# Full-height attention products and a feed-forward split in three: a two-layer transformer kernel on one Trainium2 core

## The chip, the cores and the metric

The kernel runs on one core of one Trainium2 chip. The metric is device time in microseconds of one execution, the median of several runs. Lower is better. TensorE does the matmuls (PE in the profile, with its weight loads as PEld), VectorE (DVE), ScalarE (ACT) and GpSimd (POOL) do the elementwise work, SyncE (SP) issues most DMA transfers.

## The reference

Two transformer layers over 528 rows (16 meta rows and 512 sequence rows) of width 1024, all in f32. Layer 1 has two attention branches: a windowed one (8 heads of 64, 2 key heads) and a latent one in which a small "index" network scores all keys and the best 128 are kept. Layer 2 has a differential attention (4 heads, each the difference of two softmaxes over 64-wide keys, values 128 wide) and a windowed one (8 heads of 64, 2 key heads) in which every query also sees the meta keys. Each layer mixes its branches with gates, projects them, and ends in a SwiGLU feed-forward of width 2816. Cut to what matters:

```python
# layer 1, branch a: window of 128 keys, a sink logit per head, bias by distance
s = einsum('bnqhgd,bnkhd->bnhgqk', qb, kw) * 64 ** -0.5 + bias;  o = (softmax with sink) @ vw
# layer 1, branch b: index scores choose the keys of the latent attention
logits = einsum('bqhd,bsd->bqhs', qi, ik);  score = sum_h relu(logits) * iw;  sel = top_k(score)
s = einsum('bqhc,bqkc->bqhk', q_abs, c_sel) * 64 ** -0.5 + bias;  lat = softmax(s) @ c_sel;  o = lat @ w_uv
# layer 2, branch a: differential; branch b: window of 128 to both sides and the 16 meta keys
attn = softmax(q1 k1 + bias) - lam * softmax(q2 k2 + bias);  y = attn @ v
# end of each layer
h = h + mixed @ w_out
h = h + (silu(hn @ w_gate) * (hn @ w_up)) @ w_down        # width 2816 = 22 blocks of 128
```

## The kernel before

Activations lie transposed: 128 features by columns of rows. A weight product `product(name, i, b, x)` (from line 1509) makes 128 output features: for each of the 8 (or 11, 4, 2) blocks of the contraction it runs three fp32r passes of 512 columns, since both weights and activations are split in a high part and a residual (`wh`, `wl`; `hn[:, 0]`, `hn[:, 1]`). Each weight block passes a chain: SP loads it into `stage` (line 412, after `lo` says that the residual of the last one is done), ACT copies it to `wh` (line 605, `high`), DVE or POOL subtracts to get `wl` (lines 904, 516, `low`), PE multiplies, DVE takes the result out of PSUM and sets `ev`. There are two slots, b = 0 and 1, and the phases stand in order in `PHASES` (line 82). The tiles `stage`, `wh`, `wl`, `hid` are as wide as the longest contraction, `NFH` = 11 blocks.

The feed-forward of layer l runs in two parts, a and b, of 11 blocks of the 22 each: `gu{l}a` makes 11 blocks of the hidden `hid` (gate and up product of each), `dn{l}a` multiplies them with their part of the down weights and adds the 8 output chunks into `hT`; then the same for b. PE waits in the first product of a down phase for each `hid` block in turn (`made=(hid_lo, ...)`). In the last down phase, `dn1b`, every chunk is also turned into the next layer's input on ACT and DVE (line 1356, `end_chunk`: add, gain copy and two squares on ACT, residual, sum of squares), and only then DVE makes the residual of the next weights (`low_next`); `dn2b` does a shorter form of it (line 1489).

The attention stages run units, one per block of 128 queries and head (32 for both windows and the latent one, 16 for the differential). They are interleaved over units: in turn j PE makes the scores of unit j, transposes the softmax of unit j - 2, and multiplies the transposed softmax of unit j - 3 with the values; in the window stages, quarters of the gate products of the same layer (line 1652) go between.
Heads are 64 wide, so two heads share the 128 partitions of a tile. Scores of one head use 64 rows: `r = slice(...)` selects the lower or the upper half of both operands (lines 1700 to 1703 and 1876 to 1885; the index scores, lines 1627 to 1635; the differential scores, lines 1851 to 1856). The 16 meta keys are a chunk of their own with 16 rows in the value products (lines 1677, 1717, 1773, 1868, 1902), behind a 16-column transpose (line 1666). In window attention 2 a block that doesn't begin at the first key makes its scores in two products, 16 meta columns and the rest.

## Time and profile before

| | us |
|---|---|
| median of 3 runs | 1668.69 |
| lowest, highest run | 1652.63, 1673.7 |
| the profiled execution | 1652.3 |
| its span, first to last instruction | 1650.5 |
| PE busy in it | 1607.5 |
| DVE, ACT, POOL busy | 839.7, 535.2, 203.8 |

The time outside the span is 1.8 us. The mean granted clock of TensorE over the span is 0.993 of full speed. "Busy" for PE counts the modelled, overlapping durations of pipelined matmuls; the distance between two starts is a better measure of what one takes. Idle "issue" is time in which an engine waited for nothing that the profile shows.

### The profile page before, as it was taken

The page shows a single profiled execution, that of the slowest core. Times are in us where ns is not written, and L with a number is a line of the kernel's source. Part 1 is how long each engine was busy: PE and PEld are TensorE (multiplying, and loading weights), DVE is VectorE, ACT ScalarE, POOL GpSimd, SP SyncE. Part 2 cuts the span into 40 slices and gives each one's busy share as a digit, 9 for nine tenths or more (in the row PEclk, how much of TensorE's full clock was granted, in tenths as well). Part 3 has the DMA queues.
Part 4 walks back from the last instruction along what each step waited for, and adds up shares of the span by engine and source line. Part 5 has one row for each costly group of instructions (what it writes and reads, how often), then busy time and mean ns, then how long its engine had stood idle before and what let it go on. Part 6 is the DMA issues. An engine that isn't in the chain of part 4 may idle for free.

```text
span 1650.5 us, 21586 instructions
## 1 busy us (share of the span) xinstructions
PE 1607.5 (97%) x7698; PEld 1273.5 (77%) x7698; DVE 839.7 (51%) x1579; ACT 535.2 (32%) x978; POOL 203.8 (12%) x140
## 2 busy tenths in 40 slices
PE   7899999999999999999999999999999999999997
PEld 6766776777878888888899777677777888888886
DVE  5277796436555533555554382332465554245543
ACT  4123443433322322223321363443333322122232
POOL 2222221003000000000002372221220000000000
PEclk9999999999999999999999999999999999999999
DMA  5832220003333332333232201111133333323331
GB/s 142 204 106 60 57 65 20 1 14 107 90 90 102 99 105 77 89 98 104 81 87 78 62 14 52 52 42 36 51 102 98 94 89 109 94 77 99 95 105 69
DMA packets 250508, 132.62 MB, mean 80 GB/s; under 512 B 20938, under 2 KB 247366, under 8 KB 250447
## 3 DMA queue, kind: packets, MB, share of 16 engines
q1 hardware_dynamic: 248318, 123.92, 26.5%
q0 software_dynamic: 2048, 7.77, 1.8%
q8 instruction: 37, 0.61, 0.2%
q14 instruction: 25, 0.20, 0.0%
q10 hardware_dynamic: 80, 0.14, 0.0%
HBM read 129.67 MB, written 6.38 MB: 82 GB/s over the span
## 4 chain that ended last, share of the span: by engine, by line
PE 91%; DVE 5%; DMA 2%; issue 1%; ACT 1%; POOL 0%; SPq 0%; DVEq 0%; ACTq 0%
PE psL L1529 59%; PE psL L1652 12%; PE psS L1529 4%; PE psL L1773 2%; PE psS L1902 2%; PE psT L1663 2%; PE psS L1703 1%; PE psS L1751 1%; DMA stage<-in_w_in 1%; PE psS L1717 1%; PE psL L1868 1%; PE psS L1885 1%; DMA xin<-in_x 1%; DVE W L1158 1%; PE psT L1666 1%
## 5 line engine op out<-in xcount | busy, mean ns | idle before, releaser
L1529 PE MATMUL psL<-hn,wh 128*128 128x512 f32 x1664 | 525.4, 397 | 5.2 <-POOL wl L516 5.0
L1529 PEld LDWEIGHTS psL<-hn,wh 128*128 128x128 f32 x1664 | 313.1, 189 | 82.6 <-POOL wl L516 5.2
L605 ACT ACTIVATE wh<-stage 128x1024 fp32r<-128x1024 f32 (+3 forms) x234 | 239.8, 1025 | 308.8 <-PE psL L1529 199.4
L1529 PE MATMUL psL<-hn,wl 128*128 128x512 f32 x832 | 329.8, 396 | 0.0
L904 DVE TENSOR_TENSOR wl<-stage,wh 128x1024 fp32r<-128x1024 f32 (+1 forms) x152 | 198.8, 1308 | 95.2 <-ACT wh L605 90.3
L1529 PE MATMUL psL<-hid,wh 128*128 128x512 f32 x704 | 221.3, 395 | 0.0
L516 POOL TENSOR_TENSOR wl<-stage,wh 128x1024 fp32r<-128x1024 f32 (+2 forms) x82 | 156.1, 1904 | 522.6 <-ACT wh L605 522.6
L1529 PEld LDWEIGHTS psL<-hn,wl 128*128 128x128 f32 x832 | 156.8, 188 | 36.5
L1652 PE MATMUL psL<-hn,wh 128*128 128x512 f32 x512 | 173.0, 419 | 0.0
L1529 PEld LDWEIGHTS psL<-hid,wh 128*128 128x128 f32 x704 | 132.3, 188 | 32.0
L1529 PE MATMUL psL<-hid,wl 128*128 128x512 f32 x352 | 139.2, 396 | 0.0
L1652 PEld LDWEIGHTS psL<-hn,wh 128*128 128x128 f32 x512 | 87.4, 189 | 35.7 <-issue 22.1
L1652 PE MATMUL psL<-hn,wl 128*128 128x512 f32 x256 | 101.1, 395 | 0.0
L794 ACT ACTIVATE hid<-ft 128x512 f32 (+1 forms) x44 | 27.8, 632 | 208.6 <-DVE ft L1321 208.6
L1529 PE MATMUL psS<-hn,wh 128*128 128x264 f32 x448 | 86.3, 294 | 0.7 <-DVE hn L949 0.7
L1529 PE MATMUL psL<-mix,wh 128*128 128x512 f32 x256 | 80.7, 396 | 0.9 <-DVE wl L904 0.9
L1338 DVE TENSOR_TENSOR hT<-hT,psL 128x512 f32 (+1 forms) x32 | 22.0, 688 | 112.5 <-PE psL L1529 112.5
L1529 PEld LDWEIGHTS psL<-hid,wl 128*128 128x128 f32 x352 | 66.1, 188 | 16.0
L1158 DVE CUSTOM_DVE_ANT_0 W3b<-psS,biasW,sinkb 128x272 f32<-128x272 f32 (+1 forms) x32 | 18.1, 567 | 112.1 <-PE psS L1885 82.6
L790 ACT ACTIVATE ft<-ft 128x512 f32<-128x512 f32 x44 | 27.8, 632 | 146.0 <-DVE ft L1313 146.0
L1529 PEld LDWEIGHTS psS<-hn,wh 128*128 128x128 f32 x448 | 71.8, 194 | 2.5 <-issue 1.2
L1529 PE MATMUL psS<-hn,wl 128*128 128x264 f32 x224 | 64.8, 289 | 0.0
(356 smaller groups left out, 2038.0 us busy)
## 6 DMA issues: line engine op xcount, KB each, us to landing
stage<-in_w_in SPq DMA_DIRECT2D x54, 512.0 KB, 3.8
stage<-in_w_ffn_gate SPq DMA_DIRECT2D x22, 512.0 KB, 3.8
stage<-in_w_ffn_up SPq DMA_DIRECT2D x22, 512.0 KB, 3.8
stage<-in_w_ffn_down SPq DMA_DIRECT2D x16, 704.0 KB, 4.5
stage<-in_w_ff_gate SPq DMA_DIRECT2D x22, 512.0 KB, 3.8
stage<-in_w_ff_up SPq DMA_DIRECT2D x22, 512.0 KB, 3.8
stage<-in_w_ff_down SPq DMA_DIRECT2D x16, 704.0 KB, 4.6
stage<-in_w_out SPq DMA_DIRECT2D x16, 512.0 KB, 3.8
```

The lines of the kernel that those rows point to most:

```text
L516: pool.tensor_tensor(wl[:, b, 0:n], stage[:, b, 0:n], wh[:, b, 0:n].bitcast(F32), ALU.subtract).then_inc(lo[b], 1)
L605: act.activation(wh[:, b, 0:n], stage[:, b, 0:n], ACT.Copy).then_inc(hi[b], 1)
L790: act.activation(ft[:, 1, :], ft[:, 0, :], ACT.Tanh, scale=0.5).then_inc(t_ok, 1)
L794: act.activation(hid[:, 0, bass.ds(i, 1), :], ft[:, 4, :], ACT.Copy).then_inc(hid_hi, 1)
L904: v.tensor_tensor(wl[:, b, 0:n], stage[:, b, 0:n], wh[:, b, 0:n].bitcast(F32), ALU.subtract).then_inc(lo[b], 1)
L1158: dv.link(v.tensor_tensor_reduce(out=tile, in0=scores, in1=bias, scale=1.0, scalar=least, op0=ALU.add, op1=ALU.max, accum_out=mx[:, col:co ...
L1338: v.tensor_tensor(hT[:, n, :], hT[:, n, :], psL[:, b, :], ALU.add).then_inc(ev[b], 1)
L1529: ins = pe.matmul(dst, w[:, b, k * P:(k + 1) * P], x[:, part, k, c0:c1], start=k + n == 0, stop=k == kc - 1 and n == 2)
L1652: ins = pe.matmul(psL[:, b, :], w[:, b, k * P:(k + 1) * P], hn[:, part_, k, META:], start=k + n == 0, stop=k == KD - 1 and n == 2)
L1663: ins = pe.transpose(psT[:, 0, n * P:(n + 1) * P], tile[:, col:col + P], ident[:])
L1773: ins = pe.matmul(psL[:, 0, 0:P], cn[0:w, c, :], pt, start=n == 0, stop=n == len(parts) - 1)
L1902: ins = pe.matmul(psS[:, 2 * (i % 2) + 1, h * HD:(h + 1) * HD], pt, vbn[0:w, c, h // 4 * HD:h // 4 * HD + HD], start=n == 0, stop=n == len ...
```

## The change

Scores use 128 rows. Where two key heads shared a tile (`akT`, `kbT`, and `ikT` with the same index key in both halves), the keys are now stored twice: `akz[:, g]` holds key head g in its own half of the partitions and zeros in the other half, so that the product over all 128 partitions of the query tile, which holds two heads, gives the score of one head. DVE makes these tiles, per g with a zero fill of one half and a product or copy of the other. The differential scores stay as they are.

The meta chunk of the value products uses 128 rows: the value tiles' row block of the meta keys is zero beyond row 16 (for layer 2 POOL fills it, for layer 1 that stood already), the transposed softmax too (four fills on DVE, before each stage), and the transpose takes 128 columns. In window attention 2 the meta keys also stand behind the last key, so that block 2 gets its scores in one product.

The feed-forward has three parts a, b, c of 8, 8 and 6 blocks, `NFH` is 8, and the last down phase is `dn{l}c`.

The core of the diff:

```diff
-NFH = FF // P // 2
+FPARTS = (8, 8, 6)
+NFH = max(FPARTS)
...
+def feed_forward(l):
+    return [f for ab, n in zip("abc", FPARTS) for f in ((f"gu{l}{ab}", 2 * n, KD, 1), (f"dn{l}{ab}", KD, n, 1))]
+
+def before_part(l, part):
+    return (l - 1) * sum(FPARTS) + sum(FPARTS[:part])
...
-        w, m, bias = (0, n * P, META + P) if i == 0 else (META, 0, 0)
+        w, m, bias = (0, n * P, META + P) if i == 0 else (0, n * P, META) if i == 2 else (META, 0, 0)
...
-        akT, o = at("akT", [P, NKEY], o)
+        akz, o = at("akz", [P, 2, NKEY], o)
-        ikT, o3 = at("ikT", [P, NKEY], o3)
+        ikz, o3 = at("ikz", [P, 2, NKEY], o3)
-        kbT, o = at("kbT", [P, NKEY], o)
+        kbz, o = at("kbz", [P, 2, NKEY + META], o)
...
             pool.wait_ge(ev[1], PAIR0["kv2"] + 1)
+            pool.memset(van[:, MC, :], 0.0)
+            pool.memset(vbn[:, MC, :], 0.0).then_inc(zeros, 1)
...
+            def split_keys(name, i, b, dst, again=0):
+                done(name, i, b)
+                for g in range(2):
+                    mine, other = slice(g * HD, (g + 1) * HD), slice((1 - g) * HD, (2 - g) * HD)
+                    v.memset(dst[other, g, :], 0.0)
+                    if again:
+                        v.tensor_copy(dst[mine, g, NKEY:NKEY + again], psS[mine, 2 * b, 0:again])
+                    ins = v.tensor_tensor(as_halves(dst[mine, g, 0:NKEY], NKEY), psS[mine, 2 * b:2 * b + 2, 0:NKEY // 2],
+                                          as_halves(Rk[mine, :], NKEY), ALU.mult)
+                ins.then_inc(ev[b], 1)
...
-                take_keys("kv1", i, 0, keys[2 * i])
                 if i:
+                    split_keys("kv1", i, 0, akz)
                     low_next("kv1", i, True)
+                else:
+                    take_keys("kv1", i, 0, keys[2 * i])
...
-            for n, dst in enumerate((cT, ikT)):
-                v.tensor_copy(dst[:, META:NKEY], psS[:, n, :])
-                v.tensor_copy(dst[:, 0:META], psT[:, 0, n * META:(n + 1) * META])
+            v.tensor_copy(cT[:, META:NKEY], psS[:, 0, :])
+            v.tensor_copy(cT[:, 0:META], psT[:, 0, 0:META])
+            for g in range(2):
+                mine, other = slice(g * HD, (g + 1) * HD), slice((1 - g) * HD, (2 - g) * HD)
+                v.memset(ikz[other, g, :], 0.0)
+                v.tensor_copy(ikz[mine, g, META:NKEY], psS[mine, 1, :])
+                v.tensor_copy(ikz[mine, g, 0:META], psT[mine, 0, META:2 * META])
...
+            v.memset(PTa[:, :, NEAR:], 0.0)
...
+            v.memset(PT[:, :, NB * P:], 0.0)
...
+            v.memset(PT2[:, :, NB * P:], 0.0)
...
+            v.memset(PTb[:, :, WIN2:], 0.0)
...
-                    pe.matmul(psS[:, 2 * (j % 2), 0:W], aqT[r, h % 4, i * P:(i + 1) * P], akT[r, k0:k0 + W], start=True, stop=True).then_inc(p["s"], 1)
+                    pe.matmul(psS[:, 2 * (j % 2), 0:W], aqT[:, h % 4, i * P:(i + 1) * P], akz[:, h // 4, k0:k0 + W], start=True, stop=True).then_inc(p["s"], 1)
...
-                        pe.transpose(psT[0:META, 1, 0:P], tile[:, col:col + META], ident[:])
+                        pe.transpose(psT[:, 1, 0:P], tile[:, col:col + P], ident[:])
...
-                        found.append((pt[0:META, pt.shape[-1] - P:], c, META))
+                        found.append((pt[:, pt.shape[-1] - P:], c, P))
...
-                products(f"dn{l}a", hid, made=(hid_lo, NFH * (2 * l - 2)))
-                products(f"gu{l}b", hn)
-                products(f"dn{l}b", hid, made=(hid_lo, NFH * (2 * l - 1)))
+                products(f"dn{l}a", hid, made=(hid_lo, before_part(l, 0)))
+                for part, ab in enumerate("bc", 1):
+                    products(f"gu{l}{ab}", hn)
+                    products(f"dn{l}{ab}", hid, made=(hid_lo, before_part(l, part)))
...
+                    elif k0 + W == NKEY and mcol == W:
+                        ins = pe.matmul(psS[:, 2 * (j % 2), 0:W + META], q, k[:, k0:NKEY + META], start=True, stop=True)
```

The index scores and the scores of window attention 2 change in the same way as the line of `akz`; the loops of SP, ACT and DVE over the parts follow `FPARTS`.

## Rows read from the trace of the kernel before

**Rows 1.** The page: busy time of the engines, and the chain by engine

```profile
PE 1607.5 (97%) x7698; PEld 1273.5 (77%) x7698; DVE 839.7 (51%) x1579; ACT 535.2 (32%) x978; POOL 203.8 (12%) x140
...
PE 91%; DVE 5%; DMA 2%; issue 1%; ACT 1%; POOL 0%; SPq 0%; DVEq 0%; ACTq 0%
```

**Rows 2.** Busy by stretch: length; PE, PEld, DVE, ACT, POOL; granted clock, DMA share, GB/s

```profile
0.00:129.40 129.40, 107.74 (x546) 86.21 (x546) 69.71 (x152) 38.96 (x65) 32.17 (x41) 0.95 0.58 148
129.40:223.30 93.90, 93.90 (x428) 69.73 (x428) 70.66 (x235) 38.53 (x100) 26.39 (x11) 0.98 0.22 57
223.30:257.00 33.70, 33.70 (x163) 25.95 (x161) 32.25 (x80) 13.31 (x33) 9.61 (x4) 1.00 0.21 55
277.50:357.00 79.50, 76.55 (x497) 60.50 (x496) 33.07 (x133) 36.04 (x127) 0.00 (x0) 1.00 0.00 1
937.40:998.40 61.00, 55.93 (x371) 42.05 (x371) 48.93 (x152) 37.82 (x97) 31.97 (x24) 1.00 0.03 10
998.40:1158.00 159.60, 159.60 (x775) 114.78 (x775) 44.29 (x138) 62.51 (x159) 34.60 (x15) 1.00 0.16 47
466.00:764.00 298.00, 297.89 (x1279) 239.91 (x1278) 143.16 (x166) 78.44 (x93) 0.00 (x0) 1.00 0.33 95
```

**Rows 3.** Timeline, a unit of window attention 1: start, length, engine, line, idle before

```profile
180.71 0.55 PE L1717 MATMUL psS<-avn,PTa 128*128 128x64 f32 x4
...
181.19 0.70 PE L1703 MATMUL psS<-akT,aqT 64*128 64x256 f32 x2
181.81 0.30 PEld L1652 LDWEIGHTS psL<-hn,wh 128*128 128x128 f32 x2 [0.33 <-issue]
...
182.38 0.39 PE L1652 MATMUL psL<-hn,wl 128*128 128x512 f32 x1
```

**Rows 4.** Timeline of PE, a unit of latent attention (x10 is 2 of 16 rows, 8 of 128)

```profile
336.75 0.33 PE L1763 MATMUL psL<-wuv,lat 128*128 128x64 f32 x2
337.01 1.57 PE L1773 MATMUL psL<-PT,cn 16*128 16x128 f32 x10
338.42 0.61 PE L1751 MATMUL psS<-cT,qabs 128*128 128x264 f32 x2
338.87 0.28 PE L1752 MATMUL psS<-selm,identb 128*128 128x264 bf16 x1
```

**Rows 5.** Timeline of PE, the eight 128-row value passes of the same unit alone

```profile
337.43 1.16 PE L1773 MATMUL psL<-PT,cn 128*128 128x128 f32 x8
```

**Rows 6.** Timeline of PE, a unit of window attention 2 (x6 is 2 of 16 rows, 4 of 128)

```profile
1032.07 0.39 PE L1652 MATMUL psL<-hn,wl 128*128 128x512 f32 x1
1032.39 1.02 PE L1902 MATMUL psS<-vbn,PTb 16*128 16x64 f32 x6
...
1034.75 0.40 PE L1652 MATMUL psL<-hn,wl 128*128 128x512 f32 x1
```

**Rows 7.** Timeline of PE, first two index scores, and differential scores on both halves

```profile
111.63 0.52 PE L1635 MATMUL psS<-ikT,iqT 64*128 64x144 f32 x4 [0.90 <-DVE wukT L1114]
...
969.83 0.72 PE L1855 MATMUL psS<-kaT,qaT 64*128 64x264 f32 x4
```

**Rows 8.** Timeline of DVE, end of gu1b and first chunk of dn1b

```profile
764.42 0.69 DVE L1319 TENSOR_TENSOR ft<-psL,Rk 128x512 f32<-128x512 f32 x1 [0.79 <-PE psL L1529]
...
767.39 0.91 DVE L1261 MEMSET sqacc<- 128x1024 f32 x1 [0.16 <-issue]
...
772.18 0.69 DVE L1338 TENSOR_TENSOR hT<-hT,psL 128x512 f32 x1 [2.20 <-PE psL L1529]
...
775.18 1.23 DVE L1267 TENSOR_TENSOR sqacc<-sqacc,tmp 128x1024 f32<-128x1024 f32 x1 [0.21 <-ACT tmp L816]
776.37 1.62 DVE L904 TENSOR_TENSOR wl<-stage,wh 128x1408 fp32r<-128x1408 f32 x1
```

**Rows 9.** Timeline of DVE, first chunk of dn2b

```profile
1583.17 0.69 DVE L1338 TENSOR_TENSOR hT<-hT,psL 128x512 f32 x1 [2.39 <-PE psL L1529]
...
1586.61 1.62 DVE L904 TENSOR_TENSOR wl<-stage,wh 128x1408 fp32r<-128x1408 f32 x1 [1.10 <-ACT wh L605]
```

More of the change, by code:

```diff
@@ L38 @@
 FF = 2816
-NFH = FF // P // 2
+FPARTS = (8, 8, 6)
+assert sum(FPARTS) * P == FF
+NFH = max(FPARTS)
 HD = 64
@@ L453, in layer_rest @@
                         load(f"out{l}", i, b, by_rows(wo), i * (2 * P) + b * P)
-                for half, ab in enumerate("ab"):
+                for part, ab in enumerate("abc"):
+                    f0 = sum(FPARTS[:part])
                     with sp.Fori(0, PAIRS[f"gu{l}{ab}"]) as i:
-                        load(f"gu{l}{ab}", i, 0, by_rows(wg), i * P + half * NFH * P)
-                        load(f"gu{l}{ab}", i, 1, by_rows(wu), i * P + half * NFH * P)
+                        load(f"gu{l}{ab}", i, 0, by_rows(wg), i * P + f0 * P)
+                        load(f"gu{l}{ab}", i, 1, by_rows(wu), i * P + f0 * P)
                     with sp.Fori(0, PAIRS[f"dn{l}{ab}"]) as i:
                         for b in range(2):
-                            load(f"dn{l}{ab}", i, b, by_rows(wd, half * NFH, NFH), i * (2 * P) + b * P)
+                            load(f"dn{l}{ab}", i, b, by_rows(wd, f0, FPARTS[part]), i * (2 * P) + b * P)
             layer_rest(1, win1, 1476, t["w_branch_a"][0], t["w_branch_b"][0], t["w_out"][0],
@@ L803, in _ @@
             squares_and_gain("out1", 0, ROW["ffn_norm_g"])
-            swiglu("gu1a", 0, 1)
+            swiglu("gu1a", before_part(1, 0), 1)
             only_high("dn1a")
-            swiglu("gu1b", NFH)
-            name = "dn1b"
+            swiglu("gu1b", before_part(1, 1))
+            only_high("dn1b")
+            swiglu("gu1c", before_part(1, 2))
+            name = "dn1c"
             def chunk1(i, b):
@@ L861, in _ @@
             squares_and_gain("out2", 2, ROW["norm_ffn_2"])
-            swiglu("gu2a", 2 * NFH, 1)
+            swiglu("gu2a", before_part(2, 0), 1)
             only_high("dn2a")
-            swiglu("gu2b", 3 * NFH)
-            name = "dn2b"
+            swiglu("gu2b", before_part(2, 1))
+            only_high("dn2b")
+            swiglu("gu2c", before_part(2, 2))
+            name = "dn2c"
             def chunk2(i, b):
@@ L1030, in take_scaled @@
                 v.scalar_tensor_tensor(out=dst, in0=psL[:, b, :], scalar=scale, in1=by, op0=ALU.mult, op1=ALU.mult).then_inc(ev[b], 1)
-            keys = [bkvT[:], ikwT[:], akT[:], avT[:]]
+            def split_keys(name, i, b, dst, again=0):
[8 more added lines that the diff above has]
+                ins.then_inc(ev[b], 1)
+            keys = [bkvT[:], ikwT[:], None, avT[:]]
             for i in range(2):
@@ L1350, in _ @@
             out_project(1, 0, 0, ROW["ffn_norm_g"])
-            swiglu("gu1a", 0, (2, 3))
+            swiglu("gu1a", before_part(1, 0), (2, 3))
             down("dn1a")
-            swiglu("gu1b", NFH)
+            swiglu("gu1b", before_part(1, 1))
+            down("dn1b")
+            swiglu("gu1c", before_part(1, 2))
             def end_chunk(i, b):
                 n = 2 * i + b
-                add_down("dn1b", i, b)
+                add_down("dn1c", i, b)
                 gain_low(n, 2 * i + (KD + b), g12, 0)
@@ L1362, in end_pair @@
             def end_pair(i, last):
-                low("dn1b", i, 1)
+                low("dn1c", i, 1)
                 end_chunk(i, 0)
-                low_next("dn1b", i, last)
+                low_next("dn1c", i, last)
                 end_chunk(i, 1)
@@ L1369, in _ @@
             meta_low(2)
-            pairs("dn1b", end_pair)
+            pairs("dn1c", end_pair)
             low("kv2", 0, 1)
@@ L1386, in _ @@
             v.wait_ge(R_ok, 4)
-            keys = [kaT[:, c, :] for c in range(4)] + [vaT[:, c, :] for c in range(4)] + [kbT[:], vbT[:]]
+            keys = [kaT[:, c, :] for c in range(4)] + [vaT[:, c, :] for c in range(4)] + [None, vbT[:]]
             for i in range(PAIRS["kv2"]):
@@ L1390, in _ @@
                     low("kv2", i, 1)
-                take_keys("kv2", i, 0, keys[2 * i])
+                if i == PAIRS["kv2"] - 1:
+                    split_keys("kv2", i, 0, kbz, META)
+                else:
+                    take_keys("kv2", i, 0, keys[2 * i])
                 if i:
@@ L1409, in _ @@
             v.wait_ge(nat_t, 2)
+            v.wait_ge(zeros, 2)
             for h in range(4):
@@ L1484, in _ @@
             out_project(2, 2, 2 * KD, ROW["norm_ffn_2"])
-            swiglu("gu2a", 2 * NFH, (4, 5))
+            swiglu("gu2a", before_part(2, 0), (4, 5))
             down("dn2a")
-            swiglu("gu2b", 3 * NFH)
+            swiglu("gu2b", before_part(2, 1))
+            down("dn2b")
+            swiglu("gu2c", before_part(2, 2))
             def last_pair(i, last):
-                low("dn2b", i, 1)
-                add_down("dn2b", i, 0)
+                low("dn2c", i, 1)
+                add_down("dn2c", i, 0)
                 add_squares(3, 2 * i, sqacc[:, 0, :], sq[:])
-                low_next("dn2b", i, last)
-                add_down("dn2b", i, 1)
+                low_next("dn2c", i, last)
+                add_down("dn2c", i, 1)
                 add_squares(3, 2 * i + 1, sqacc[:, 0, :], sq[:])
             clear_squares()
-            pairs("dn2b", last_pair)
+            pairs("dn2c", last_pair)
             new_rms(5)
```

25 lines of the change are left out of this document (11 added, 14 removed).

## Prediction

> **What bounds the kernel now.** I read the page's busy shares and its chain first [rows 1]: the reader is to see that the chain that ended last is TensorE (PE) for 91%, so the time is mostly the sum of what PE streams plus its switching. Then the busy table by stage [rows 2]. In the sliding-window attention of layer 1 (129 to 257 us) and of layer 2 (998 to 1158 us) PE is busy for the whole stretch, in the latent attention (277 to 357) for 76.55 of 79.50 us, in the feed-forward for all of it. The differential attention (937 to 998) is mixed: PE 55.93, DVE 48.93 of 61.00 us. In the last quarter of window attention 1 DVE is busy for 32.25 of 33.70 us, a second bound close behind PE. "Busy" hides stalls, since matmul ends are modelled, so the third view is the timeline of single units [rows 3 to 6], where the distance between starts is what counts.
>
 So the other seven take 0.78, 0.11 us each. Two 264-column score passes of 128 rows take 0.45 (338.42 to 338.87), 0.22 each. A 512-column pass is 298 us / 1279 = 0.23, in the stretch from 466 us [rows 2]. These are the unstalled prices.
>
> Now a unit of window attention 1 [rows 3]: four value passes, two 64-row score passes, two gate passes take 180.71 to 182.38 = 1.67 us. Unstalled they are 0.39 + 0.44 + 0.46 = 1.29 (the first 64-column value pass takes 0.06, the other three 0.11: the weight load sets it). The rest, 0.38 us, is two switches of height: the weight load of the other height comes late, and its row puts the idle 0.33 down to "issue", not to a semaphore. A 16-row meta chunk in the latent stage [rows 4]: two output passes, two meta passes, eight value passes take 336.75 to 338.42 = 1.67; unstalled 12 x 0.11 less 0.05 = 1.27; the switches cost 0.40. Window attention 2 has both [rows 6]: from the last gate pass at 1032.07 to the third one after it at 1034.75 is 2.68; unstalled 0.23 (gate) + 0.06 + 7 x 0.11 (second meta pass, values, 16-column scores) + 2 x 0.22 + 2 x 0.23 = 1.96. Saved per unit: 0.72.
>
> **Gains, stage by stage.** Columns and passes stay, only the height changes, and score passes of 64 and of 128 rows stream alike.
> - Window attention 1: 24 units x 0.38 = 9.1, and 0.34 (0.72 less 0.38) for the meta chunk of the first 8 = 2.7. In the last 8 units DVE leaves at most 33.70 - 32.25 = 1.4 of their 3.0; I take 1.0. Sum 12.8.
> - Latent: 32 x 0.40 = 12.8; its early units already wait on others in part (PE 76.55 of 79.50), so I take 11.
> - Window attention 2: 32 x 0.72 = 23.0, with DVE at 44.29 of 159.60 and ACT at 62.51. Block 2's meta columns join its main score product: two 16-column passes x 0.11 x 8 units = 1.8. Sum 24.8.
> - Differential: its scores keep half height; only the meta chunk changes, 16 x 0.40 = 6.4, between 0 (DVE sets the pace, at 80% and in bursts) and 6.4: I take 3.
>
> Gains: 51.6 us.
>
> **Costs.**
> (a) The index scores lose an overlap. Four 64-row passes of 144 columns on opposite halves take 0.52 us busy [rows 7]. At full height they go end to end: later by 0.2 in the small block, by 0.9 (four passes of 0.22) in the large. ReLU on ACT takes the units one by one anyway, so between 0 and 4 x 0.6 = 2.4; I take 0.5, as the switches around the three q products go too.
> (b) The padded index keys are made on DVE between the key transposes and the first index score, where PE waits (idle 0.90, released by DVE) [rows 7]: two zero fills of 528 columns and one more copy of 512. A fill of 1024 columns takes 0.91 [rows 8], so 0.47 each; the copy, like the 512-column add at 772.18, 0.69: 1.6 us, all on the path.
> (c) The window keys of layer 1 get the same and push one weight residual 1.5 us later, so also the reload of its buffer; PE still has a product to run then: between 0 and 1.5, I take 0.5. Layer 2's are behind a product of PE: 0; without that cover, 1.6.
> (d) Four zero fills of 256 strided columns, 0.25 each on DVE at the head of a stage: 0.8 together. The two on POOL run after its long wait, ahead of work that needs ACT first: 0, without that cover about 1.
> (e) FFN. Weights, passes and bytes are the same in all; per layer there are 8 more accumulations into hT (0.69 each [rows 8]; DVE is busy 143 of 298 us), 8 more loads on SP and conversions on ACT, all of narrower blocks, and one more wait of PE for a last hid chunk. That chunk is ready some 3.0 us after the last up product (764.42 to the fill at 767.39) [rows 8], and PE needs it 3 x 0.23 x (n - 1) after it: 4.8 us for n = 8, 3.45 for n = 6: no stall. What does not shrink is the end of the layer. In the last down part of layer 1 DVE does per chunk [rows 8]: add (772.18), wait for ACT's copy and two squares (till 775.18), add squares, residual of the next weights (from 776.37, 1.62 us for 1408 columns). At 768 columns the residual lies between a 512-column pass (0.69) and a 1024-column one (1.23): 0.96. The cycle is then 776.37 - 772.18 + 0.96 = 5.15 us, while PE needs 18 x 0.23 = 4.14 (it was 5.8 against 7.6). DVE becomes the bound: 1.0 us x 6 chunks, 1.0 for the second chunk (its residual stands behind the 0.91 fill), 0.6 at the end: 8 us; late next is the head of the keys of layer 2. In layer 2 only one square is taken [rows 9]: 1586.61 - 1583.17 = 3.44, less 0.5 for ACT's narrower conversion, plus 0.96 = 3.9, below 4.14; the way back to PE adds some 0.14 a chunk, and the fill 0.9: 2 us. Together 10, between 4 and 16.
>
> Costs: 0.5 + 1.6 + 0.5 + 0.8 + 10 = 13.4 us.
>
> **Sum.** 51.6 - 13.4 = 38 us. The profiled execution took 1652.3, so 1614 on its own terms. It stands at the low end of the three runs, whose median, 1668.7, is 1.0% above it; from there the sum is 1631. Two of the three runs lie high, so I take **1626 us**. The gain at best: 51.6 + 3.4 + 1.8 less costs of 7.4 = 49; at worst 38 - 3 - 6 - 2 = 27. The case's own range is 1604 to 1645.
>
> **A rule that speaks against it.** Half-height passes on opposite halves overlap: four of 264 columns in the differential stage take 0.72 busy, where two of full height take 0.61 [rows 4, 7]. The Trainium skill, "TensorE: Matmul & The Clock Gate", Part 3 (Packing small matmuls), says that matmuls in distinct row groups run concurrently, and advises to place small contractions so; the trace agrees where such products are neighbours. By that rule the index scores would lose their whole overlap: an estimate of 2 us more than I count, a gain of 36. In the window stages no two score products are neighbours [rows 3, 6], and nothing is lost.
>
> **Rivals.**
> 1. *Other engines take the gain.* DVE or ACT sets the pace in more units (window 1 from its third block, all of differential, early latent: 3 + 3 + 5 us), and the short down part loses 1.7 instead of 1.0 a chunk (6 us): 38 - 17 = 21, 1631 to 1648. For it: 32.25 of 33.70. Against: PE busy throughout elsewhere. Chance 0.16.
> 2. *The change doesn't do what it says:* the gaps around short products are semaphore waits, so full height leaves them and only the costs remain, 1666 to 1682. Against: inside one accumulation, with no wait between its chunks, the 16-row passes take 0.21 instead of 0.11 [rows 4, 5]. Chance 0.05. The skill's same page, Part 2 (LDWEIGHTS), lets a load run ahead into the background weights, by which there would be nothing to gain; the rows show this only between equal heights.
> 3. *Slower, by the clock.* PE would idle more in the latent and differential stages. If the granted clock fell there from 2.4 to 1.2 GHz, as parts of the first 129 us must have (mean 0.95) [rows 2], their PE time (66 + 53 us after the change) would double: +119 - 38, over 1725; from some 70 us at half clock on it is slower by 2%. Against: both stages stand at 1.00 now with 3 and 5 us idle. Chance 0.03.
> 4. *More is gained:* differential gives 6, the FFN ends cost 3: 48 us, 1604 to 1621. Chance 0.08.
>
> **How the numbers follow.** A difference of 2% (33 us) is about what a measurement of this kernel can tell from none. My case has 0.68; of its span 27 to 49 about a sixth lies under 33, so 0.57 faster, 0.11 the same. With rival 4, 0.65 faster; with rivals 1 and 2, 0.32 the same; 0.03 slower. The range 1602 to 1650 takes in my case at either level of the runs, rivals 4 and 1, and leaves out rivals 2 and 3 and some ends.
>
> **What would show it.** Right: window 2 units 0.7 us shorter with no "issue" idle ahead of the first gate weight load; meta passes 0.11 apart; DVE without gaps in the last eight units of window 1; PE idle about 1 us per chunk in dn1c, waiting for wl, little in dn2c; the first index score 1.6 us later after the transposes. Wrong: 0.2 us gaps that stay at full height, a lower clock in the latent stage, or PE waiting in the 8-wide parts.

## The result, and the profile after

The changed kernel takes 1617.74 us (median of 4 runs, 1616.44 to 1618.78); the kernel before took 1669.21 us beside it (4 runs, 1652.63 to 1673.7). The ratio is 0.9709, 95% interval 0.9642 to 0.9776: faster by more than 2%, as forecast, and inside the range of 1602 to 1650, 8 us below the 1626 that I named. The profiled execution of the changed kernel took 1618.78 us, its span is 1617.0. Against the profiled execution of before the gain is 33.5 us, where I had summed 38; between the medians it is 51.5 us. The two differ for a reason that I had not foreseen (experiments 1, 4 to 7 and 9 to 12).

The page of the changed kernel: busy time by engine, and the chain that ended last [rows 1].

```profile
PE 1563.0 (97%) x7682; PEld 1271.6 (79%) x7682; DVE 861.4 (53%) x1627; ACT 537.4 (33%) x994; POOL 204.1 (13%) x142
...
PE 84%; DVE 9%; issue 2%; DMA 2%; ACT 2%; POOL 0%; SPq 0%; DVEq 0%; ACTq 0%
```

PE still sets the end, with 16 instructions fewer and 44.5 us less "busy"; DVE's share of the chain went from 5% to 9%. Where, the table by stage tells (columns as in [rows 2]); the last two lines are the feed-forward of layer 1, ahead of its last down part and in it.

```profile
131.80:214.50 82.70, 82.70 (x432) 69.37 (x433) 71.83 (x237) 37.60 (x100) 26.38 (x11) 1.00 0.25 65
214.50:252.00 37.50, 34.86 (x178) 28.68 (x177) 35.66 (x87) 14.15 (x35) 9.56 (x4) 1.00 0.20 56
269.80:340.00 70.20, 65.38 (x478) 54.28 (x478) 32.88 (x133) 35.12 (x124) 0.00 (x0) 1.00 0.00 1
928.20:986.00 57.80, 51.22 (x370) 41.89 (x370) 49.49 (x152) 37.78 (x97) 30.51 (x24) 1.00 0.04 10
986.00:1124.00 138.00, 137.80 (x760) 114.94 (x758) 45.79 (x139) 61.38 (x157) 35.93 (x15) 1.00 0.19 54
530.50:776.90 246.40, 246.40 (x1057) 198.74 (x1056) 111.85 (x130) 61.04 (x72) 0.00 (x0) 1.00 0.32 93
776.90:817.10 40.20, 35.69 (x146) 26.38 (x144) 28.48 (x35) 19.94 (x31) 0.00 (x0) 1.00 0.27 79
```

In the last units of window 1 DVE is busy for 35.66 of 37.50 us and PE no longer for the whole stretch; the latent stage leaves PE 4.8 us idle (it was 2.95); the last down part leaves it 4.5. Window 2 is as full of PE as before, and 21 us shorter.

Between the first score of window 1 and the first latent one each of the two profiled executions has a stretch at half clock, at different places, and in the table below they nearly cancel. In the kernel before it is at the head of window 1:

```profile
130.50:133.90 3.40, 3.40 (x9) 2.10 (x8) 2.45 (x13) 0.69 (x3) 2.22 (x1) 0.50 0.01 2
```

In the changed kernel it is as long and begins at 252.6 us, at the tail of window 1.

The same comparison from one stage's first product to the next one's, read from the two timelines. The third column is what my sum gives, each cost in its place:

| stretch | before us | after us | difference | my sum |
|---|---|---|---|---|
| start to first score of window 1 | 129.38 | 131.76 | +2.4 | +2.1 |
| to first latent score | 148.19 | 138.03 | -10.2 | -12.1 |
| to last latent score | 73.25 | 66.59 | -6.7 | -10.8 |
| branch, FFN 1, to first differential score | 586.60 | 591.84 | +5.2 | +8 |
| to first score of window 2 | 60.98 | 57.83 | -3.2 | -2.8 |
| to its last score | 156.88 | 135.81 | -21.1 | -24.6 |
| FFN 2, to the end | 495.20 | 495.12 | -0.1 | +2 |
| sum | 1650.5 | 1617.0 | -33.5 | -38 |

Timeline of PE in the changed kernel: a unit of window 1 [rows 3], of the latent stage [rows 4] and of window 2 [rows 6].

```profile
170.45 0.55 PE L1763 MATMUL psS<-avn,PTa 128*128 128x64 f32 x4
170.84 0.65 PE L1749 MATMUL psS<-akz,aqT 128*128 128x256 f32 x2
171.14 0.81 PE L1699 MATMUL psL<-hn,wh 128*128 128x512 f32 x2
171.78 0.40 PE L1699 MATMUL psL<-hn,wl 128*128 128x512 f32 x1
...
331.26 0.33 PE L1809 MATMUL psL<-wuv,lat 128*128 128x64 f32 x2
331.43 1.33 PE L1819 MATMUL psL<-PT,cn 128*128 128x128 f32 x10
332.60 0.39 PE L1797 MATMUL psS<-cT,qabs 128*128 128x264 f32 x1
...
1007.83 0.40 PE L1699 MATMUL psL<-hn,wl 128*128 128x512 f32 x1
1008.07 0.78 PE L1950 MATMUL psS<-vbn,PTb 128*128 128x64 f32 x6
1008.68 0.35 PE L1932 MATMUL psS<-kbz,qbT 128*128 128x16 f32 x2
1008.87 0.68 PE L1933 MATMUL psS<-kbz,qbT 128*128 128x256 f32 x2
1009.20 0.81 PE L1699 MATMUL psL<-hn,wh 128*128 128x512 f32 x2
1009.85 0.40 PE L1699 MATMUL psL<-hn,wl 128*128 128x512 f32 x1
```

The window 1 stretch, four value passes to the third gate pass, is 170.45 to 171.78 = 1.33 us (1.67 before); the latent one 331.26 to 332.60 = 1.34 (1.67); the window 2 one 1007.83 to 1009.85 = 2.02 (2.68), for the two excursions in it. Each excursion to another height and back had cost 0.33 us, in all three stages. I had 0.38, 0.40 and 0.36. The weight load of the first gate pass, which had 0.33 us of "issue" idle ahead of it [rows 3], has none:

```profile
170.78 0.30 PEld L1749 LDWEIGHTS psS<-akz,aqT 128*128 128x128 f32 x2
171.11 0.41 PEld L1699 LDWEIGHTS psL<-hn,wh 128*128 128x128 f32 x2
```

What PE and its weight loads waited for in the changed kernel: in start-up, at the end of window 1, in the latent stage (two lines) and in the last down part of layer 1 (us in total, times, longest).

```profile
PE psS L1682 <- DVE wukT L1150: 3.1, 1, 3.1
...
PE psL L1699 <- DVE tmp L1177: 1.9, 1, 1.9
...
PE psT L1713 <- ACT PT L732: 1.9, 5, 0.8
...
PEld psT L1713 <- ACT W L716: 5.6, 10, 1.0
...
PE psL L1577 <- DVE wl L922: 4.1, 7, 0.9
```

The first was 0.90 before [rows 7]: the padded index keys' fills and copy, 2.2 us. The second is new: DVE at the tail of window 1. The third and fourth are the latent stage's waits for ACT: PE for its copies of the transposed weights (0.9 us in one wait before), the weight loads of the transposes for its exponentials (1.7 us in three before). The fifth is the short down part. Timeline of DVE there, one chunk [rows 8]:

```profile
795.00 1.23 DVE L1305 TENSOR_TENSOR sqacc<-sqacc,tmp 128x1024 f32<-128x1024 f32 x1 [0.23 <-ACT tmp L832]
796.14 0.95 DVE L922 TENSOR_TENSOR wl<-stage,wh 128x768 fp32r<-128x768 f32 x1
797.01 0.68 DVE L1376 TENSOR_TENSOR hT<-hT,psL 128x512 f32 x1
799.03 0.75 DVE L1310 SCALAR_TENSOR_TENSOR hn<-hT,g,hn  x1 [1.33 <-ACT hn L830]
800.01 1.23 DVE L1305 TENSOR_TENSOR sqacc<-sqacc,tmp 128x1024 f32<-128x1024 f32 x1 [0.23 <-ACT tmp L832]
```

From one chunk to the next it takes 800.01 - 795.00 = 5.0 us (I had 5.15), where PE needs 4.14. The residual of 768 columns takes 0.95 (I had 0.96).

### The profile page after: what moved, and what is told of

It is laid out like the page before. It is cut to its first block, busy times and chain, and to the rows that moved or that the text cites. A ratio compares the mean times of both kernels' runs of the same rounds, so it can differ in the third digit from the quotient of the medians.

```text
span 1617.0 us, 21794 instructions
## 1 busy us (share of the span) xinstructions
PE 1563.0 (97%) x7682; PEld 1271.6 (79%) x7682; DVE 861.4 (53%) x1627; ACT 537.4 (33%) x994; POOL 204.1 (13%) x142
## 4 chain that ended last, share of the span: by engine, by line
PE 84%; DVE 9%; issue 2%; DMA 2%; ACT 2%; POOL 0%; SPq 0%; DVEq 0%; ACTq 0%
PE psL L1577 57%; PE psL L1699 10%; PE psS L1577 5%; PE psT L1710 1%; PE psL L1819 1%; PE psS L1950 1%; DVE W L1194 1%; PE psS L1797 1%; DMA stage<-in_w_in 1%; DMA xin<-in_x 1%; DVE acc L1188 1%; PE psT L1713 1%; DVE st L1187 1%; PE psS L1749 1%; DVE wl L922 1%
## 5 line engine op out<-in xcount | busy, mean ns | idle before, releaser
L1577 PEld LDWEIGHTS psL<-hn,wh 128*128 128x128 f32 x1664 | 313.3, 189 | 82.3 <-POOL wl L528 5.3
L619 ACT ACTIVATE wh<-stage 128x1024 fp32r<-128x1024 f32 (+3 forms) x250 | 243.2, 973 | 341.9 <-PE psL L1577 238.4
L1699 PEld LDWEIGHTS psL<-hn,wh 128*128 128x128 f32 x512 | 92.2, 190 | 21.2 <-issue 2.0
L808 ACT ACTIVATE hid<-ft 128x512 f32 (+1 forms) x44 | 27.8, 632 | 210.2 <-DVE ft L1359 210.2
L1376 DVE TENSOR_TENSOR hT<-hT,psL 128x512 f32 (+1 forms) x48 | 32.9, 686 | 104.3 <-PE psL L1577 104.3
L804 ACT ACTIVATE ft<-ft 128x512 f32<-128x512 f32 x44 | 27.8, 632 | 150.0 <-DVE ft L1351 150.0
```

The source lines that it names most:

```text
L619: act.activation(wh[:, b, 0:n], stage[:, b, 0:n], ACT.Copy).then_inc(hi[b], 1)
L804: act.activation(ft[:, 1, :], ft[:, 0, :], ACT.Tanh, scale=0.5).then_inc(t_ok, 1)
L808: act.activation(hid[:, 0, bass.ds(i, 1), :], ft[:, 4, :], ACT.Copy).then_inc(hid_hi, 1)
L1376: v.tensor_tensor(hT[:, n, :], hT[:, n, :], psL[:, b, :], ALU.add).then_inc(ev[b], 1)
L1577: ins = pe.matmul(dst, w[:, b, k * P:(k + 1) * P], x[:, part, k, c0:c1], start=k + n == 0, stop=k == kc - 1 and n == 2)
L1699: ins = pe.matmul(psL[:, b, :], w[:, b, k * P:(k + 1) * P], hn[:, part_, k, META:], start=k + n == 0, stop=k == KD - 1 and n == 2)
```

## The experiments

Twelve kernels. The executions of some of them fall into two groups, one with a mean granted clock of about 0.99 and one of about 0.98, 18 us apart in the kernel before. Of 52 executions of the kernel before beside these runs, 36 stand at 0.98 (median 1671) and 16 at 0.99 (median 1653). The profiled execution of before belongs to the second group, the median of its runs to the first.

### 1. The kernel before, once more

The file is unchanged.

> The kernel before, unchanged, as a yardstick of what two runs of one program differ by. Its four runs so far span 1652.6 to 1673.7 us, those of the changed kernel 1616.4 to 1618.8. Theory: the profiled execution (1652.3) is a lucky one and the others lose about 16 us in some stage; then a trace of a 1669 us execution shows that stage, most likely as a stretch with the granted clock at half or as a stall ahead of the first scores. Rival: the spread is spread over all stages, nothing to be seen. Ratio 1.00 in both.

Measured: 1671.65 us, ratio 1.0033 (0.9975 to 1.0091); 8 of 10 executions at the lower clock, and the profiled one is among them. Busy by stretch (columns as in [rows 2]): the first 5.9 us of the latent stage and the 37.5 us after them, first in this execution,

```profile
278.40:284.30 5.90, 4.69 (x31) 3.33 (x30) 3.14 (x17) 2.92 (x14) 0.00 (x0) 1.00 0.00 0
284.30:321.80 37.50, 37.50 (x135) 29.62 (x135) 10.23 (x46) 10.52 (x47) 0.00 (x0) 0.50 0.00 1
```

then in the execution of before that stands ahead of the prediction,

```profile
277.50:283.40 5.90, 4.69 (x31) 3.33 (x30) 3.14 (x17) 2.92 (x14) 0.00 (x0) 1.00 0.00 0
283.40:320.90 37.50, 37.50 (x235) 28.88 (x236) 17.39 (x73) 18.27 (x72) 0.00 (x0) 1.00 0.00 1
```

and in the changed kernel.

```profile
275.70:313.20 37.50, 36.13 (x259) 28.95 (x258) 18.99 (x80) 19.27 (x74) 0.00 (x0) 1.00 0.01 1
```

The same program did the same 31 matmuls in the same 5.90 us; then in one execution the granted clock was 0.50 (1.2 GHz) for 37.5 us and 135 matmuls got done, in the other it stayed at 1.00 (2.4 GHz) and 235 did. First to last latent score takes 89.90 us in the one and 73.25 in the other: 16.65 us, most of the 18 between the groups. The changed kernel's four executions stand at 0.991 to 0.995. So the 51.5 us between the medians are 35 at an equal clock (1653 to 1617.7) and 16 from the clock, if the executions without a profile lost their time in the same place, as their clock and time suggest. The next question was which part of the change holds the clock.

### 2. The feed-forward parts alone

The kernel before with the three parts and their loops; scores over 64 rows and meta chunks of 16 as they were.

```diff
-NFH = FF // P // 2
+FPARTS = (8, 8, 6)
+NFH = max(FPARTS)
```

> The kernel before with the feed-forward in parts of 8, 8 and 6 alone; keys, meta chunk and transposes as before. Theory (the short last part makes DVE the bound in dn1c): slower than before by 6.5 us in layer 1 and 1.4 in layer 2 as the changed kernel's trace has it (40.1 and 35.0 us for 144 passes that stream in 33.6), sum 8 us, ratio 1.005. Rival (the split costs nothing, and the gain in attention is smaller than I think): 0 to 2 us, ratio 1.000.

Measured: 1669.47 us, ratio 1.003 (0.9972 to 1.0088). The share of low executions was smaller (5 of 10, against 15 of 25 of the kernel before beside it, a difference that chance can make), which hides the cost; at equal clock it is 1659 against 1653 and 1678 against 1671: 6 to 7 us. By stage: from last latent to first differential score 593.0 (586.6 before), window 2's last score to the end 496.4 (495.2). I had 8 + 2.

### 3. The narrow part first

```diff
-FPARTS = (8, 8, 6)
+FPARTS = (6, 8, 8)
```

> The changed kernel with the parts in the order 6, 8, 8, so that the last down part is 8 wide. Theory: DVE's cycle per chunk is 5.15 + 0.27 = 5.4 us, PE needs 24 x 0.23 = 5.5, so PE no longer waits: 6 to 8 us less than the changed kernel, 1610 us. The 6-wide part at the front has no extra work on DVE and loses nothing. Rival (each change from one part to the next costs, not the width of the last): as the changed kernel, 1617.

Measured: 1612.87 us, ratio 0.9662 (0.9591 to 0.9733), 4.9 us below the changed kernel (the spans of the two profiles: 1612.3 and 1617.0). Layer 1's stretch is 587.9 us instead of 591.8, layer 2's 493.6 instead of 495.1 (586.6 and 495.2 in the kernel before, the same sum within 0.3). The page's group for the hid products shows the wait gone; in this run, and then in the changed kernel:

```profile
L1577 PE MATMUL psL<-hid,wh 128*128 128x512 f32 x704 | 221.7, 396 | 0.2
```

```profile
L1577 PE MATMUL psL<-hid,wh 128*128 128x512 f32 x704 | 222.5, 397 | 4.7 <-DVE wl L922 4.7
```

The feed-forward's cost is the order of its parts, not their number: a last part of 6 blocks gives PE too little work for DVE's cycle of 5.0 us, one of 8 (24 x 0.23 = 5.5 us of PE a chunk) gives enough, though its residual of 1024 columns takes DVE 1.22 us instead of 0.95. There DVE waits for PE, in run 3:

```profile
788.44 1.22 DVE L922 TENSOR_TENSOR wl<-stage,wh 128x1024 fp32r<-128x1024 f32 x1
789.90 0.69 DVE L1376 TENSOR_TENSOR hT<-hT,psL 128x512 f32 x1 [0.24 <-PE psL L1577]
```

### 4. Meta chunks back at 16 rows in all four stages

The four zero fills of the transposed weights go too.

```diff
-pe.transpose(psT[:, 1, 0:P], tile[:, col:col + P], ident[:])
+pe.transpose(psT[0:META, 1, 0:P], tile[:, col:col + META], ident[:])
-found.append((pt[:, pt.shape[-1] - P:], c, P))
+found.append((pt[0:META, pt.shape[-1] - P:], c, META))
```

> The changed kernel with the meta chunk back at 16 rows in all four stages (and without the four zero fills on DVE): only the scores have 128 rows. Theory (each change of height costs about 0.19 us each way): window 2 units 0.33 us longer than in the changed kernel (32 x 0.33 = 10.6), latent 6 to 7 us, window 1 2.7, differential 3, less 0.8 for the fills: 21 to 23 us slower than the changed kernel, 1639 us. Rival (score products carry the gain, the meta chunk little, since one accumulation holds no wait): below 8 us slower, 1625.

Measured: 1659.71 us, ratio 0.9974 (0.9924 to 1.0025). Nine of ten executions stand at 0.98, one at 0.991 with 1644.78. The profiled one is a low one:

```profile
272.80:278.80 6.00, 4.79 (x31) 3.41 (x31) 3.14 (x17) 3.00 (x15) 0.00 (x0) 1.00 0.00 0
278.80:316.30 37.50, 37.50 (x135) 29.59 (x135) 10.24 (x46) 10.57 (x47) 0.00 (x0) 0.50 0.00 1
```

Window 1 from first to last score takes 112.8 us (110.2 padded, 123.8 before), window 2 145.3 (135.8 and 156.9). So the change of the scores gives 11.0 and 11.6 us, the meta chunk 2.6 and 9.5. Not all of the first two is height: about 1.4 us of the 11.0 is the half clock at the head of window 1 in the kernel before, and about 1.5 of the 11.6 is block 2's joined product, which this run keeps (its units gain 5.65 - 5.14 = 0.51 us, those of block 1 0.33). Of the rest of the difference to the changed kernel, 23.3 us are the latent stage, 89.9 instead of 66.6, and 5.4 the differential one, where the granted clock was at half for 10.2 us too (the changed kernel's stands above, with 1.00):

```profile
957.00:1021.00 64.00, 59.62 (x370) 44.47 (x371) 50.20 (x155) 38.40 (x99) 32.80 (x24) 0.92 0.03 9
```

In the latent stage the padded meta chunks keep the clock; the scores don't.

### 5. The latent stage alone at 16 rows

The changed kernel, with a number of rows as argument, which only the latent stage gives; its zero fill goes.

```diff
-transposed(p, j - 2, units[j - 2][3], W3[:, (j - 2) % 3, :])
+transposed(p, j - 2, units[j - 2][3], W3[:, (j - 2) % 3, :], META)
-parts = pieces(units[u][3], PT[:, u % 2, :])
+parts = pieces(units[u][3], PT[:, u % 2, :], META)
```

> The changed kernel with one thing undone: in the latent stage alone the meta chunk is 16 rows high again (transposes to 16 rows, value passes over 16 rows, no zero fill); window 1, differential and window 2 stay padded, parts 8, 8, 6. Theory A (the 16-row passes of the latent stage let its granted clock fall): besides the 6.7 us of the switches the stage shows a stretch of some 37 us at half clock, first to last latent unit takes about 90 us instead of 66.6, and the median is about 1618 + 23 = 1641. Theory B (the clock falls for what stands before it, the half-height passes of window 1 or of the whole kernel): the stage takes 73 us at full clock and the median is about 1624.

Measured: 1626.47 us (1624.53 to 1629.14, 4 runs), clocks 0.989 to 0.992; the stage takes 73.26 us. The number of theory B. The latent stage with its 16-row passes, behind the first 5.9 us:

```profile
274.10:311.60 37.50, 37.50 (x235) 28.83 (x236) 17.50 (x73) 18.18 (x71) 0.00 (x0) 1.00 0.01 1
```

Taken alone it says that 16-row passes in the latent stage aren't enough.

### 6. The kernel before, with the latent stage alone padded

The same on the kernel before, with a zero fill of the transposed weights ahead of the stage.

```diff
-transposed(p, j - 2, units[j - 2][3], W3[:, (j - 2) % 3, :])
+transposed(p, j - 2, units[j - 2][3], W3[:, (j - 2) % 3, :], P)
-parts = pieces(units[u][3], PT[:, u % 2, :])
+parts = pieces(units[u][3], PT[:, u % 2, :], P)
+v.memset(PT[:, :, NB * P:], 0.0)
```

> The kernel before with one thing added: the latent stage's meta chunk padded to 128 rows; all else as before (half-height scores, 16-row meta chunks elsewhere, parts 11, 11). Theory A (the latent stage's own 16-row passes let its clock fall): the stage takes some 66.6 us in nearly every execution, none of them at half clock, and the median is 1650.5 - 6.7 = 1644, 25 us under the kernel before. Theory B (what stands before the stage does it): most executions keep the 37 us at half clock, and the median is about 1671 - 7 = 1664.

Measured: 1647.02 us (1646.33 to 1648.74, 4 runs), ratio 0.9858 (0.9836 to 0.988), all four at 0.989 to 0.992, the stage at 66.61 us, beside seven executions of before that all stood at 0.976 to 0.984. The number of theory A: but for one zero fill everything ahead of the stage is as before, and with its own meta chunk padded the clock stays.

```profile
285.00:322.50 37.50, 36.12 (x259) 28.90 (x257) 18.97 (x80) 19.31 (x74) 0.00 (x0) 1.00 0.01 1
```

These few lines in one stage are worth 24 us of the median, 7 of them from the switches. Runs 5 and 6 together say that the 16-row passes must be there and that something else must come to them.

### 7. Meta chunks of 64 rows

```diff
-pe.transpose(psT[:, 1, 0:P], tile[:, col:col + P], ident[:])
+pe.transpose(psT[0:HD, 1, 0:P], tile[:, col:col + HD], ident[:])
-found.append((pt[:, pt.shape[-1] - P:], c, P))
+found.append((pt[0:HD, pt.shape[-1] - P:], c, HD))
```

> The changed kernel with the meta chunk 64 rows high instead of 128 in all four stages (16 of the 64 rows hold keys, the others zeros); scores stay at full height. Theory A (any change of height costs the same, because the next weight load then starts late): unit times are those of the run with 16-row chunks, window 2 takes 145 us and window 1 112.8, together about 13 us more than the changed kernel at one clock, latent 73 us. Theory B (the price goes with the rows left out): 64 of 112 rows back give about half of it, window 2 some 141 us, window 1 111.6. For the clock: if it falls with every change of height, the latent stage takes 90 us and the median is about 1660; if 64 rows are enough to keep it, about 1641.

Measured: 1643.86 us (4 runs, clocks 0.990 to 0.992). Window 1 112.8 us, window 2 145.1, latent 73.5: theory A to the digit. Timeline of PE, the latent unit of before [rows 4] in this run:

```profile
332.19 0.33 PE L1809 MATMUL psL<-wuv,lat 128*128 128x64 f32 x2
332.46 1.57 PE L1819 MATMUL psL<-PT,cn 64*128 64x128 f32 x10
333.87 0.39 PE L1797 MATMUL psS<-cT,qabs 128*128 128x264 f32 x1
```

Ten passes take 333.87 - 332.46 = 1.41 us, as with 16 rows (337.01 to 338.42), and 1.17 with 128. What costs is that the height changes, not how far. As to the clock, 64 rows kept it in four of four, with PE as busy and its products as many as in the kernel before:

```profile
278.70:316.20 37.50, 37.50 (x235) 29.19 (x235) 17.27 (x73) 18.24 (x72) 0.00 (x0) 1.00 0.01 1
```

So the change of height as such doesn't always bring a fall; but run 5, with 16 rows, kept the clock in four of four too, and this run alone doesn't tell 64 rows from 16.

### 8. The best of these together

The index keys are stored once again, and the index scores run over 64 rows.

```diff
-FPARTS = (8, 8, 6)
+FPARTS = (6, 8, 8)
-ikz, o3 = at("ikz", [P, 2, NKEY], o3)
+ikT, o3 = at("ikT", [P, NKEY], o3)
-q = iqT[:, h // 2, i * P:(i + 1) * P]
+r = slice(h % 2 * HD, h % 2 * HD + HD)
+q = iqT[r, h // 2, i * P:(i + 1) * P]
```

> The changed kernel with parts 6, 8, 8 and the index scores at half height again (their padded copy of the index keys gone), all other parts of the change kept. Theory: parts 6, 8, 8 give 5 us (1612.9 in the run with that alone), and the padded index keys cost 1.6 us of fills and copy ahead of the first index score and about 0.5 of lost overlap: a median of about 1611. Rival: the half-height scores leave two switches of height at each q product and give the overlap back, 1613.

Measured: 1608.39 us (1606.2 to 1610.15), ratio 0.9632 (0.9608 to 0.9656), against 0.9662 for run 3. PE's wait ahead of the first index score is 0.9 us again instead of 3.1. It is the fastest kernel here, 9 us below the changed one. What the index keys alone are worth is not separated: in its profiled execution the clock also stayed up behind that wait (1.00 over 110 to 120 us, 0.66 in the changed kernel), and run 3's interval (0.9591 to 0.9733) takes in this ratio.

### 9 and 10. Run 5, a little later in time

One fill ahead of the padded index keys in run 9, two in run 10.

```diff
+for _ in range(1):
+    dv.link(v.memset(ikz[:, 0, :], 0.0))
```

> The run with the latent stage alone at 16 rows (median 1626, latent stage 73.3 us at full clock), with one zero fill more on DVE ahead of the first index score: the same work, everything after it some 0.6 us later. Theory C (16-row passes in the latent stage let its clock fall when the stage's head happens to lie badly in time): at least some executions show some 37 us at half clock in the latent stage and take about 1644, the others 1627. Theory B (16-row or half-height passes are needed in window 1 as well): all executions take 1626 to 1628.

> As the run before it, with two zero fills more, some 1.2 us later. Theory C: at least some executions of this or of the one before take about 1645, with the latent stage at some 90 us. Theory B: all take 1626.5 to 1629.

Measured: 1629.29 us (1627.28 to 1642.0) and 1630.77 us (1628.81 to 1647.98). In each, three of four executions stand at 0.988 to 0.990, and one at 0.981 (1642.0) and 0.978 (1647.98), 14 and 18 us above the others' median. Theory B said never. The two low executions weren't profiled; that they lost it in the latent stage is inferred from their clock and time.

### 11. The kernel before, a little later in time

```diff
+for _ in range(3):
+    dv.link(v.memset(ikT[:], 0.0))
```

> The kernel before with three useless zero fills on DVE ahead of the first index score, so that all that follows is about 1.8 us later. Theory C: the share of executions that lose 17 us to half clock in the latent stage changes; where it goes to none the kernel is faster with the added work, 1652 instead of 1671. Theory B: the share stays, and the median is about 1671 + 2 = 1673.

Measured: 1673.36 us, ratio 1.0031 (0.9988 to 1.0075); 8 of 10 executions at the lower clock, 10 of 13 of the kernel before beside them. The profiled execution is a low one, its latent stage again at half clock for 37.5 us. The share didn't move: theory C's second half is not borne out, and where in time the stage begins is not shown to be what decides.

### 12. The 16-row value passes left out

Run 4, with a line more in the latent stage.

```diff
 parts = pieces(units[u][3], PT[:, u % 2, :])
+parts = [q for q in parts if q[1] != MC]
```

> The run with 16-row meta chunks in all four stages (median 1660, nine of its ten executions with some 37 us at half clock in the latent stage), with the latent stage's 16-row value passes left out: the latent output lacks the meta keys' part, 64 passes fewer, no change of height left in the stage's products. Theory A (the 16-row value passes, with the switches around them, are what lets the clock fall): no execution falls, the stage takes 66 us or less, median about 1644.8 - 7 - 2 = 1636. Theory D (it falls for too little work at the stage's head, whatever the height): with fewer passes it falls at least as often, the stage takes over 80 us, median about 1655.

Measured: 1628.88 us (1628.43 to 1630.87, 4 runs), clocks 0.991 to 0.994, where run 4 had nine of ten at 0.98 and the kernel before, beside this run, four of seven. The stage takes 62.4 us (I had 66 or less). Less work for PE doesn't bring the clock down; taking the 16-row passes out keeps it up. The same unit once more:

```profile
332.21 0.33 PE L1805 MATMUL psL<-wuv,lat 128*128 128x64 f32 x2
332.38 1.11 PE L1816 MATMUL psL<-PT,cn 128*128 128x128 f32 x8
333.33 0.39 PE L1793 MATMUL psS<-cT,qabs 128*128 128x264 f32 x1
```

Without the meta chunk the unit takes 333.33 - 332.21 = 1.12 us, with it 1.34 at 128 rows and 1.67 at 16. The chunk cost 0.55 us as it was and costs 0.22, its two passes, as it is.

**What the runs on the clock settle.** In the kernels without 16-row value passes in the latent stage (the changed one, runs 3, 6, 7, 8 and 12) none of 24 executions stands at the lower clock. With them it is 36 of 52 of the kernel before, 30 of 40 in runs 1, 2, 4 and 11, and 2 of 12 in runs 5, 9 and 10. So the fall was seen with these passes only; they don't bring it by themselves. The weight lies on runs 6 and 12: there all else ahead of the stage is as in kernels that fall often (seven of seven executions of the kernel before beside run 6, nine of ten of run 4), and none of their eight falls, with a zero fill ahead of the stage in the one and without it in the other. Against the 2 of 12 with window 1 padded, the 0 of 16 of the others prove little. It isn't where they ran: the kernel before stood at the lower clock in seven of seven executions beside run 5, and in ten of thirteen beside runs 9 and 10. Why the share is so much smaller when window 1's meta chunk (and that of the later stages) is padded stays open.

The differential stage must be kept apart. In ten of the fourteen profiled executions (not in those of the kernel before, the changed one, runs 3 and 8) its granted clock too was at half, for 7 to 10 us, whether its meta chunk had 16 or 64 rows (62.0 to 63.4 us from its first score to the first of window 2, instead of 61.0) or 128 (60.2 in runs 5, 9 and 10, instead of 57.8). In run 5, with 128 rows:

```profile
936.90:947.10 10.20, 10.20 (x35) 7.13 (x34) 6.99 (x25) 5.38 (x15) 0.00 (x0) 0.50 0.00 1
```

There padding doesn't keep the clock, and what brings it down was not tested.

## Why the prediction was right, and where it was not

**What bounds the kernel.** Right. PE's stream and its switching set the time, and taking the switches away shortened it stage by stage.

**The price of a switch.** The mechanism was right, rival 2 fell: inside one accumulation, where nothing is waited for, ten passes went from 1.41 to 1.17 us. The size was a little high: 0.33 an excursion, not 0.36 to 0.40. My unstalled reference was at fault: it counted each narrow pass at its best spacing of 0.11, and at equal heights the unit still takes 1.34 us in the latent stage for my 1.27, and 1.33 in window 1 for my 1.29. The Trainium skill, "TensorE: Matmul & The Clock Gate", Part 2 (LDWEIGHTS), says that the time of a weight load goes with its columns and not with its rows; the traces agree, the loads of the latent value passes take 182 ns with 16 rows and 190 with 128 in the kernel before, and 184 with 64 in run 7. The same part of the Trainium skill has PE pull a load ahead when it goes to the background weights; in these traces that is seen between equal heights only (idle ahead of the load 0.33 us after 64 rows [rows 3], none after 128), which is what the change lives on.

**Window 1.** I took 12.8 and had 10.2. The 31 steps from first to last score gained 13.6, of which about 1.4 is the clock: the first two steps, at half clock in the kernel before, shrank by 1.01 and 1.16, the third by 0.40. The units of the last quarter run at 3.88 us like the others, but for one of 4.86 in which PE waited 0.8 us for ACT: DVE didn't slow them all, as I had said it would, but ran late behind them, and PE waited for it once, 1.9 us, at the end. Behind that idle the clock was at half for 3.4 us, which cost another 1.5 (the same stretch takes 26.3 us in runs 5 and 8, without that, and 27.8 here). DVE as second bound was right, its place was not.

**Latent.** The step that failed most: 6.7 for 11. Only the units with wide scores keep the whole 0.33; in the early ones PE now waits for ACT. The weight loads of the transposes wait 5.6 us for its exponentials, 1.7 before: the 3.9 between are as much as is missing from 32 x 0.33 = 10.6. Of PE itself only 1.9 more of idle time are seen (4.8 us in the stage, 2.95 before). I had allowed 1.8 us for that, from the idle time of the kernel before, and it is rival 1 in small.

**Window 2.** 21.1 for 24.8. Units of block 0 went from 5.10 to 4.44 us and those of block 1 from 5.45 to 4.79, 0.66 for my 0.72; those of block 2 from 5.65 to 4.79, 0.86 for 0.94. The first three units gain 0.8 together, since they don't hold both excursions yet.

**Differential.** 3.2 for 3: at half of the 6.4, ACT and DVE took the rest (PE waits 4.2 us for ACT's copies, 3.2 before).

**Costs.** Start-up 2.4 for 2.1, with DVE's 2.2 seen in PE's wait; it varies by up to 2.4 from one execution to another (128.5 to 130.9 us in the kernel before and runs 1, 2 and 6, 131.1 to 132.6 in the changed one and runs 3 to 5, 7 and 12). The feed-forward 5.2 - 0.1, or 7.6 in run 2 by itself, for 10. In the 8-wide parts of layer 1 PE never waited (246.40 of 246.40 us in the stretch shown), as predicted; in the last part of layer 1 it lost 4.1 us in 7 waits, as predicted in place and cause.

**From the sum to the median.** This is the step that was wrong without my seeing it. I put the changed kernel's median where that of before stood, about 1% over the profiled execution, and so raised 1614 to 1626. But the high executions of before are high because their latent stage runs for 37.5 us at 1.2 GHz (runs 1 and 11 show it), and the change takes that away: its median lies at its profiled execution. The errors have opposite signs, +4.5 us in the terms against -12 for the group, and leave 8. The clear verdict is in part luck as well: at an equal clock the gain is 35 us, 2.1%, hardly more than the 2% asked for, and the other 16 came from a cause that the prediction doesn't have. Rival 3 had looked at the right stage and the right quantity with the wrong sign: I argued that less work would cost the clock, and run 12, with the least work of all, kept it. In the differential stage a fall did come in other runs, as it feared, but it cost 1.0 to 2.4 us and not 53.

## What to carry to other kernels

Among short products, count the changes of row height before the columns: here each excursion cost 0.33 us whether the other height was 16 or 64 rows, and zero rows that make the heights equal cost PE only their passes; where another engine has to make them on the path, as the index keys, count that too (2.2 us). Put the narrowest part of a split loop where the other engines have slack, not at the end, where each chunk has more to do (5 us here for a change of order). Before scaling a sum to a median, ask what the runs above the profiled execution do differently: if their granted clock is lower, find the stage, and ask whether the change touches it.

## What the runs showed of the hardware

In two executions of one program the granted clock of the latent stage was at half for 37.5 us in one and at full in the other, after the same 31 matmuls in the same 5.9 us; PE was busy throughout that stretch, and got 135 matmuls done in it instead of 235. By their mean clock and time, most executions of that program (36 of 52) are of the first kind. Such executions were seen only with kernels that have 16-row value passes in the stage, in none of the 20 executions with them at 64 or 128 rows nor of the four without them. That holds for this stage alone: in the differential stage the clock fell for 7 to 10 us with 128-row passes too. The cost was 16.65 us, less than half of the stretch: work that takes 37.5 - 16.65 = 20.9 us at full clock took 37.5 at half. By what path 16-row passes come to weigh on the clock is not shown by any of these runs.
